# Gate rows by way of a DRAM row and ScalarE's DMA queue, in place of diagonal products on TensorE

## The chip, the cores and the metric

One core of a Trainium2 chip runs the whole program. Its engines are TensorE (PE in the profile; its weight loads are PEld), VectorE (DVE), ScalarE (ACT), GpSimd (POOL) and SyncE (SP). SP and ACT each issue DMAs to a queue of their own (q1 and q10 in the profile), and both queues use the same 16 DMA engines. The metric is the time of one execution on the device in microseconds; three runs of the kernel before took 3442.11, 3445.48 and 3447.05 us, median 3445.48.

## The reference, cut to what matters

Two networks run one after the other, both in fp32, on 256 tokens of 1024 values. The first (two layers of gated FFNs and a mixer of SSD, mLSTM and RWKV heads) is not touched by the change. The second has two layers, works on the 256 tokens and, until its last mixer, on 256 context tokens too, and every branch is scaled by a gate before it is added. The gates are six-fold products of the condition with `ada_w`:

```
m_lat = split((silu_c  @ ada_w[l] + ada_b[l])[:, None, :], 9)     # 9 vectors of 1024, for the tokens
m_ctx = split( silu_cc @ ada_w[l] + ada_b[l], 9)                  # the same for the context
def half_ffn(t, m, j):
    h = modulate(rmsnorm(t, norm_g[l, j]), m[3 * j], m[3 * j + 1])
    return t + 0.5 * m[3 * j + 2] * swiglu_2(h, w_gate, w_up, w_down)
x = half_ffn(x, m_lat, 0);  ctx = half_ffn(ctx, m_ctx, 0)
y_lat, y_ctx = fourier_layer(...)      # layer 0; retention_layer(...) in layer 1
x = x + m_lat[5] * y_lat;   ctx = ctx + m_ctx[5] * y_ctx
x = half_ffn(x, m_lat, 2);  ctx = half_ffn(ctx, m_ctx, 2)
```

A gate is one vector of 1024 values, the same for every token.

## The kernel before, in words

**Where a gate is needed.** A branch's result lies in PSUM with tokens on the 128 partitions and features along the free dimension, 512 to a bank. To scale it, `Gated.vector` (L705) multiplies a bank by `gb`, in which the gate row stands on all 128 partitions, and adds the product to the residual rows. The gates themselves come out of the ada stage (L432) the other way round: `K.mods[:, l, c, n]` holds feature 128c + p of condition n on partition p.

**How the row is spread before.** `Gates` (L648) turns it in pieces of 512 values, here called gate rows. For each, DVE makes four diagonal matrices of 128x128 (`ident` times the column of `mods`, times 0.5 in the half-FFNs, L667), PE multiplies each by a matrix of ones into a bank (`ps`, L681), and ACT copies the bank to `gb` (L691). Six stages have gates: half00, half02 and half10 (the half-FFNs on 512 rows, layer and place in the name) and the Fourier mixer with 2 conditions, so 4 gate rows each; the retention output (tile names ret...) and half12, the last half-FFN, with 1 condition, so 2 gate rows each.

**Order of the work.** Each stage is a generator for each engine, and one list, `order`, fixes how stages alternate: each entry lets one stage take its next step on all four engines (L337). An engine executes its instructions in that order, and a wait holds all that stands behind it on the same engine. In `ffn` (L2953) a step of the half-FFN (one gate-and-up tile: 48 products of 512 columns, or of 256 in half12) is followed by two steps of ada while ada still has work (in half00 and half02), and then by one step of the gates, until these are used up. Fourier and the retention output have their gates' steps written into the order by hand (L3123, L3156).

**Weights.** SP's queue loads tiles of 128x2048 fp32 into a ring of buffers (L319). Each is split in two for PE: ACT writes the high part (`hi`, L310, 1.92 us), DVE the low part (`lo`, L316, 2.29 us), and PE multiplies with both. There are two `hi` buffers in most stages, three in half12. `plan` (L221) puts each split at a place in `order`: `early` before, `late` behind the step of that entry. An ada step on DVE is a set of running sums over a loaded tile (`acc`, L464).

## Time and profile before

| what | value |
|---|---|
| three runs, lowest, median, highest | 3442.11, 3445.48, 3447.05 us |
| profiled execution, first to last instruction (span) | 3442.6 us; no time of its own beside the span is shown, which stands 2.9 us below the median of the runs |
| PE busy | 3305.7 us, 96% |
| DVE busy | 2101.4 us, 61% |
| ACT busy | 1308.7 us, 38% |
| mean granted clock of PE | 0.989 |
| HBM traffic | 459 MB read, 1.05 MB written, 134 GB/s over the span |

Busy time is a share over the whole span; the chain of waits tells which engine set the end. Matmuls overlap one another in the records, so a single duration of a product is longer than the distance to the next one, and the cost of a few products is better read from the distance between marks on either side.

### The profile page before, as it was taken

The numbers are of one execution on the slowest core, as the hardware profiler recorded it, in microseconds if no ns is written. First come the engines' busy times: TensorE is split into PE (matmuls) and PEld (weight loads), VectorE is DVE, ScalarE is ACT, GpSimd is POOL, SyncE is SP. The second block draws the span as 40 slices with busy tenths as digits, with TensorE's granted clock in tenths as the row PEclk, the third lists the DMA queues.
The fourth block names the chain that finished last, engine by engine and source line by source line (L and its number), as shares of the span: only waits on it lengthen the run. The fifth ranks groups of instructions, "written<-read, shape, count | busy, mean of one in ns | idle before, by whom it ended". The sixth has DMA issues, their size and how long they took to land.

```text
span 3442.6 us, 47741 instructions
## 1 busy us (share of the span) xinstructions
PE 3305.7 (96%) x19896; PEld 2886.8 (84%) x19896; DVE 2101.4 (61%) x2545; ACT 1308.7 (38%) x1584; POOL 115.9 (3%) x126
## 2 busy tenths in 40 slices
PE   7998999999999899999999999999999999999998
PEld 7988887998988888798888877888878888787897
DVE  6767657777776667678774855763353333544654
ACT  4444244444435234544421223322232222444443
POOL 0001200000000211000000000000000000000000
PEclk9999999999999999999999999999999999999999
DMA  6542021565553022455443531343222222323452
GB/s 247 235 178 74 27 96 67 204 239 197 236 208 117 27 71 74 171 230 217 147 165 122 179 119 38 134 141 104 87 93 90 93 97 73 126 99 109 165 184 98
DMA packets 83842, 463.08 MB, mean 135 GB/s; under 512 B 7573, under 2 KB 11285, under 8 KB 43562
## 3 DMA queue, kind: packets, MB, share of 16 engines
q1 hardware_dynamic: 77952, 451.45, 35.9%
q10 hardware_dynamic: 5674, 8.57, 0.8%
q8 instruction: 157, 2.57, 0.3%
q14 instruction: 59, 0.48, 0.0%
HBM read 458.95 MB, written 1.05 MB: 134 GB/s over the span
## 4 chain that ended last, share of the span: by engine, by line
PE 66%; DVE 24%; ACT 6%; issue 2%; DMA 0%; POOL 0%; DVEq 0%; ACTq 0%; POOLq 0%
PE ps L100 66%; DVE lo L316 8%; DVE acc L464 5%; ACT hi L310 3%; PE ps L557 1%; DVE acc L461 0%; DVE m0restMs L2004 0%; DVE m1restMs L2004 0%; DVE xt L712 0%; DVE ct L712 0%; DVE half00fin L710 0%; DVE f20rot L886 0%; DVE f21rot L886 0%; DVE f10rot L886 0%; DVE f11rot L886 0%
## 5 line engine op out<-in xcount | busy, mean ns | idle before, releaser
L316 DVE TENSOR_TENSOR lo<-raw,hi 128x2048 fp32r<-128x2048 f32 (+1 forms) x357 | 809.6, 2268 | 627.9 <-ACT hi L310 606.2
L310 ACT ACTIVATE hi<-raw 128x2048 fp32r<-128x2048 f32 (+1 forms) x357 | 676.0, 1894 | 578.1 <-PE ps L100 547.5
L464 DVE SCALAR_TENSOR_TENSOR acc<-raw,sil,acc 128x512 f32<-128x512 f32 x504 | 379.0, 752 | 20.4
L100 PE MATMUL ps<-half00hs,hi 128*128 128x512 f32 x672 | 209.4, 393 | 0.9 <-DVE lo L316 0.9
L100 PE MATMUL ps<-half02hs,hi 128*128 128x512 f32 x672 | 209.1, 392 | 1.0 <-DVE lo L316 1.0
L100 PE MATMUL ps<-half10hs,hi 128*128 128x512 f32 x672 | 208.5, 391 | 1.0 <-DVE lo L316 1.0
L100 PEld LDWEIGHTS ps<-half10hs,hi 128*128 128x128 f32 x672 | 125.7, 188 | 28.5 <-DVE lo L316 1.9
L100 PEld LDWEIGHTS ps<-half02hs,hi 128*128 128x128 f32 x672 | 125.5, 188 | 28.6 <-DVE lo L316 1.9
L100 PEld LDWEIGHTS ps<-half00hs,hi 128*128 128x128 f32 x672 | 125.1, 188 | 28.0 <-DVE lo L316 1.8
L100 PE MATMUL ps<-half02hs,lo 128*128 128x512 f32 x352 | 137.9, 392 | 0.0
L100 PE MATMUL ps<-half00hs,lo 128*128 128x512 f32 x352 | 137.6, 391 | 0.0
L100 PE MATMUL ps<-half10hs,lo 128*128 128x512 f32 x352 | 137.5, 391 | 0.0
L100 PE MATMUL ps<-half12hs,hi 128*128 128x256 f32 x704 | 127.2, 283 | 2.1 <-DVE half12hs L636 2.1
L100 PE MATMUL ps<-hi,half00hf 128*128 128x512 f32 x352 | 110.7, 394 | 2.1 <-DVE mods L474 1.4
L100 PE MATMUL ps<-hi,half02hf 128*128 128x512 f32 x352 | 110.4, 394 | 1.5 <-DVE mods L474 1.5
L100 PEld LDWEIGHTS ps<-half12hs,hi 128*128 128x128 f32 x704 | 109.3, 191 | 3.0 <-DVE half12hs L636 1.8
L100 PE MATMUL ps<-hi,half10hf 128*128 128x512 f32 x352 | 109.2, 390 | 0.0
L100 PE MATMUL ps<-f10hs_h,hi 128*128 128x256 f32 x352 | 101.5, 288 | 7.3 <-DVE lo L316 7.2
L100 PE MATMUL ps<-f21hs_h,hi 128*128 128x256 f32 x352 | 100.9, 287 | 5.5 <-DVE lo L316 3.8
L100 PE MATMUL ps<-msk 128*128 128x128 f32 x886 | 104.5, 276 | 1.0 <-PE ps L2819 1.0
L100 PEld LDWEIGHTS ps<-msk 128*128 128x128 f32 x886 | 102.4, 192 | 3.3 <-PE ps L2819 1.2
L100 PE MATMUL ps<-f20hs_h,hi 128*128 128x256 f32 x352 | 100.8, 286 | 3.2 <-DVE f20hs_l L636 1.5
(921 smaller groups left out, 8019.5 us busy)
## 6 DMA issues: line engine op xcount, KB each, us to landing
raw<-in_ffn_w_gate_up SPq DMA_DIRECT2D x88, 1024.0 KB, 9.0
raw<-in_ffn_gu SPq DMA_DIRECT2D x88, 1024.0 KB, 4.8
raw<-in_ffn_w_down SPq DMA_DIRECT2D x85, 1024.0 KB, 5.2
raw<-in_ada_w SPq DMA_DIRECT2D x72, 1024.0 KB, 4.9
raw<-in_w_in_t SPq DMA_DIRECT2D x28, 1024.0 KB, 4.9
raw<-in_ret_w_in SPq DMA_DIRECT2D x24, 1024.0 KB, 4.8
raw<-in_w_out SPq DMA_DIRECT2D x16, 1024.0 KB, 4.9
raw<-in_w_in_n SPq DMA_DIRECT2D x12, 1024.0 KB, 4.8
```

The source lines that it names most:

```text
L100: return p().matmul(o, l, r, start=start, stop=stop, skip_group_check=True)
L310: a().activation(self.high(w), self.raw[self.place(r)][:, 0:width], ACT.Copy).then_inc(*a.mark(self.wac, w))
L316: v().tensor_tensor(self.low(w), self.raw[self.place(r)][:, 0:width], self.high(w).bitcast(F32), ALU.subtract).then_inc(*v.mark(self.wdv, w))
L464: v().scalar_tensor_tensor(out=acc[:, n, :], in0=w[:, k, :], scalar=s, in1=acc[:, n, :], op0=ALU.mult, op1=ALU.add).then_inc(*v.mark(self. ...
L557: x = p().transpose(b[:, t * 128:(t + 1) * 128], self.xs[:, 2 * s + t, c * 128:(c + 1) * 128], K.ident)
```

## The change

`Gates` no longer uses PE or PSUM. DVE writes the whole gate vector of the stage, scaled, into a small SBUF tile `gcol` (128 partitions, 8 or 16 values of use), once for each stage. ACT's queue writes each condition's 1024 values from there to a row in DRAM, waits until these writes have landed, and then issues one DMA that reads the row or rows back to all 128 partitions of `gb`. The stage that uses the gates waits for that. `Gates` has 2 steps where it had 5 or 3, so the later steps leave `order`; the first two stand where they stood. PE's waits for the gates to have left their bank go, and the DMA scratch of the program is set to 4096 bytes.

```diff
@@ class Core
+        self.gcol = m.take("gcol", 2, 8)
@@ class Gates
-        self.l, self.j, self.rows, self.phases, self.half = l, j, 2 * n, 2 * n + 1, half
-        self.gb, self.dg, self.bank = gb, dg, bank
+    phases = 2
+        self.row = K.nc.dram_tensor(who + "row", (n, 1024), F32, kind="Internal").ap()
+        self.out, self.back = Loads(K.sem(who + "out"), n), Loads(K.sem(who + "back"))
     def vector(self, v):
-        for i in range(self.rows):
-            ...
-            for m in range(4):
-                v().tensor_scalar(self.dg[:, m, :], K.ident, K.mods[:, self.l, c, n:n + 1], self.half, ALU.mult, ...)
-            yield
-        yield
+        if self.before:
+            v.wait_ge(*self.before.out.all)
+        v.wait_ge(*K.ada.dv["mods", 18 * self.l + 17])
+        v().tensor_scalar(K.gcol, K.mods[:, self.l, at:at + 8, :].rearrange("p c n -> p n c"), self.half, None,
+                          ALU.mult).then_inc(*v.mark(self.dv, "gc"))
+        yield
+        yield
-    def tensor(self, p):
-        ...
-            for m in range(4):
-                x = mm(p, b[:, m * 128:(m + 1) * 128], self.K.ones, self.dg[:, m, :])
     def scalar(self, a):
         self.enter(a)
-        yield
-        for i in range(self.rows):
-            a.wait_ge(*self.pe["sum", i])
-            a().activation(self.gb[:, n, q * 512:(q + 1) * 512], self.K.ps[self.bank][:, :], ACT.Copy)...
-            yield
+        a.wait_ge(*self.dv["gc"])
+        for n in range(self.n):
+            a().dma_start(self.row[n].rearrange("(c p) -> p c", p=P), K.gcol[:, n, :],
+                          allow_slow_non_contiguous=True).then_inc(*self.out.mark())
+        yield
+        a.wait_ge(*self.out.all)
+        a().dma_start(self.gb, self.row.rearrange("n k -> (n k)").unsqueeze(0).broadcast_to([P, 1024 * self.n]).rearrange(
+            "p (n k) -> p n k", n=self.n)).then_inc(*self.back.mark())
+        yield
     def done(self, e):
-        e.wait_ge(*self.ac["gb", self.rows - 1])
+        e.wait_ge(*self.back.all)
@@ class Ffn, tensor
-            if self.finish.gates:
-                self.finish.gates.done(p)
@@ class Fourier, tensor
-                    if t == 3:
-                        self.finish.gates.done(p)
@@ network
-    for s in (half, half, four, half, half, four, gates, four, gates, four, four, four, gates, four, gates, four, gates):
+    for s in (half, half, four, half, half, four, gates, four, gates, four, four, four, four, four):
@@ retention output
-        if q < 3:
+        if q < 2:
             run(gates)
@@ kernel
+    nc = _bacc.Bacc("TRN2", target_bir_lowering=False, num_devices=1, dynamic_dma_scratch_size=4096)
```

ACT's instructions at the start of half00, before and after the change (`hi` from `raw` is a weight split, `half00rot` and `half00hf` belong to the half-FFN's first tiles):

```order
L864 ACTIVATE half00hf_241<-half00rot 128x512 [waits s_ffn_act,s_ffn_dve]
L310 ACTIVATE hi_65<-raw_49 128x2048 [waits s_ffn_act,s_ring0,s_norm_dve]
L860 ACTIVATE half00rot<-ps 128x512 [waits s_w_hi,s_ffn_pe]
L864 ACTIVATE half00hf_241<-half00rot 128x512 [waits s_ffn_act,s_ffn_dve]
L691 ACTIVATE half00gb<-ps 128x512 [waits s_ffn_act,s_gate_pe]
L310 ACTIVATE hi_66<-raw_55 128x2048 [waits s_gate_act,s_ring6]
```

```order
L850 ACTIVATE half00hf_241<-half00rot 128x512 [waits s_ffn_act,s_ffn_dve]
L675 DMA half00grow<-gcol 128x8x1 [waits s_ffn_act,s_gate_dve,s_norm_dve]
L675 DMA half00grow<-gcol 128x8x1
L311 ACTIVATE hi_65<-raw_49 128x2048 [waits s_ring0]
L846 ACTIVATE half00rot<-ps 128x512 [waits s_w_hi,s_ffn_pe]
L850 ACTIVATE half00hf_241<-half00rot 128x512 [waits s_ffn_act,s_ffn_dve]
L679 DMA half00gb<-half00grow 128x2048 [waits s_ffn_act,s_half00gout]
L311 ACTIVATE hi_66<-raw_55 128x2048 [waits s_ring6]
```

The two writes, with their wait for DVE's `gcol` (s_gate_dve), stand ahead of a weight split now, and the read back with its wait for the writes (s_half00gout) stands ahead of the next one. The same holds in half02, half10 and half12.

ACT in the retention output, where `ys_h` is the split of the retention's result:

```order
L2433 ACTIVATE ys_h<-retyT 128x1024 [waits s_out_act] x3
L310 ACTIVATE hi_65<-raw_52 128x2048 [waits s_out_act,s_ring3]
L691 ACTIVATE retgb<-ps 128x512 [waits s_w_hi,s_gate_pe]
L310 ACTIVATE hi_66<-raw_53 128x2048 [waits s_gate_act,s_out_pe,s_ring4]
L691 ACTIVATE retgb<-ps 128x512 [waits s_w_hi,s_gate_pe]
```

```order
L2419 ACTIVATE ys_h<-retyT 128x1024 [waits s_out_act] x3
L675 DMA retgrow<-gcol 128x8x1 [waits s_out_act,s_gate_dve]
L311 ACTIVATE hi_65<-raw_52 128x2048 [waits s_ring3]
L679 DMA retgb<-retgrow 128x1024 [waits s_w_hi,s_retgout]
L311 ACTIVATE hi_66<-raw_53 128x2048 [waits s_out_pe,s_ring4]
```

Here too the write comes between `ys_h` and the first split, and the read back between the first split and the second.

ACT in the Fourier stage, from the squares of the second half (`fxs,st<-ct`) on; `fZ` are results of the first transform, `fsin` and `fs_h` belong to the second:

```order
L2621 ACTIVATE fxs,st<-ct 128x512 [waits s_four_act] x4
L2586 ACTIVATE fZ<-ps 128x257 [waits s_four_act,s_four_pe] x4
L2606 ACTIVATE fwx_257<-fwx 5x1024 [waits s_four_act,s_four_second]
L691 ACTIVATE four_gb<-ps 128x512 [waits s_four_act,s_gate_pe]
L2628 ACTIVATE fxs<-ct,st 128x512 [waits s_gate_act,s_four_pool]
L2628 ACTIVATE fxs<-ct,st 128x512 [waits s_four_act,s_four_pool]
L2593 ACTIVATE fsin<-ps 128x256 [waits s_four_act,s_four_pe] x2
```

```order
L2605 ACTIVATE fxs,st<-ct 128x512 [waits s_four_act] x4
L675 DMA fourgrow<-gcol 128x8x1 [waits s_four_act,s_gate_dve]
L675 DMA fourgrow<-gcol 128x8x1
L2570 ACTIVATE fZ<-ps 128x257 [waits s_four_pe]
L2570 ACTIVATE fZ<-ps 128x257 [waits s_four_act,s_four_pe] x3
L2590 ACTIVATE fwx_256<-fwx 5x1024 [waits s_four_act,s_four_second]
L679 DMA four_gb<-fourgrow 128x2048 [waits s_four_act,s_fourgout]
L2612 ACTIVATE fxs<-ct,st 128x512 [waits s_four_pool]
L2612 ACTIVATE fxs<-ct,st 128x512 [waits s_four_act,s_four_pool]
L2577 ACTIVATE fsin<-ps 128x256 [waits s_four_act,s_four_pe] x2
```

The writes stand ahead of the four `fZ` copies, the read back ahead of `fxs` and `fsin`; the three later gate copies are gone.

## Rows read from the trace of the kernel before

**Rows 1.** The page, part 4: engines' shares of the chain that ended last.

```profile
PE 66%; DVE 24%; ACT 6%; issue 2%; DMA 0%; POOL 0%; DVEq 0%; ACTq 0%; POOLq 0%
```

**Rows 2.** The chain in order of time: start, us, what.

```profile
2561.18 175.14 PE ps L100 x782
```

**Rows 3.** Tile half10dg: duration ns min/median/max, first and last start.

```profile
L667 DVE TENSOR_SCALAR half10dg<-msk,mods x16: 285/286/289, 2570.6 to 2606.0; 128x128 f32<-128x128 f32 x16
```

**Rows 4.** Timeline, ACT in half10: start us, us, instruction, [idle before].

```profile
2578.65 0.60 ACT L860 ACTIVATE half10rot<-ps 128x512 f32<-128x512 f32 x1 [6.88 <-PE ps L100]
...
2590.44 0.60 ACT L860 ACTIVATE half10rot<-ps 128x512 f32<-128x512 f32 x1 [7.10 <-PE ps L100]
...
2659.04 0.60 ACT L860 ACTIVATE half10rot<-ps 128x512 f32<-128x512 f32 x1 [6.93 <-PE ps L100]
...
2669.92 0.60 ACT L860 ACTIVATE half10rot<-ps 128x512 f32<-128x512 f32 x1 [6.88 <-PE ps L100]
```

**Rows 5.** Timeline, ACT's queue: DMA issues.

```profile
23.23 0.44 ACTq L413 DMA_DIRECT2D mask<-in_c_mask  x1
...
240.20 0.60 ACTq L1064 DMA_DIRECT2D m0small<-in_rwkv_g_up  x1
```

**Rows 6.** Timeline, half00: ACT, DVE, then PE.

```profile
1671.94 1.92 ACT L310 ACTIVATE hi<-raw 128x2048 fp32r<-128x2048 f32 x1
...
1678.77 1.25 DVE L667 TENSOR_SCALAR half00dg<-msk,mods 128x128 f32<-128x128 f32 x4
1680.13 2.29 DVE L316 TENSOR_TENSOR lo<-raw,hi 128x2048 fp32r<-128x2048 f32 x1
...
1683.18 0.71 PE L100 MATMUL ps<-half00hs,hi 128*128 128x512 f32 x2
...
1696.75 0.71 PE L100 MATMUL ps<-half00hs,hi 128*128 128x512 f32 x2
```

**Rows 7.** Timeline, half02: DVE, then PE.

```profile
2182.69 1.25 DVE L667 TENSOR_SCALAR half02dg<-msk,mods 128x128 f32<-128x128 f32 x4
...
2187.33 0.70 PE L100 MATMUL ps<-half02hs,hi 128*128 128x512 f32 x2
```

**Rows 8.** Timeline, half12: DVE, then ACT.

```profile
3254.53 1.26 DVE L667 TENSOR_SCALAR half12dg<-msk,mods 128x128 f32<-128x128 f32 x4
...
3270.02 0.38 ACT L860 ACTIVATE half12rot<-ps 128x256 f32<-128x256 f32 x1 [2.03 <-PE ps L100]
```

**Rows 9.** Timeline, retention output: ACT, DVE, then PE.

```profile
3187.70 1.92 ACT L310 ACTIVATE hi<-raw 128x2048 fp32r<-128x2048 f32 x1
...
3189.71 1.26 DVE L667 TENSOR_SCALAR retdg<-msk,mods 128x128 f32<-128x128 f32 x4
...
3194.24 0.48 PE L100 MATMUL ps<-hi,ys_h 128*128 128x512 f32 x1
```

**Rows 10.** The DMA view: queues (packets, MB, share), issues (KB each, us to landing).

```profile
q1 hardware_dynamic: 77952, 451.45, 35.9%
q10 hardware_dynamic: 5674, 8.57, 0.8%
...
out<-xt SPq DMA_DIRECT2D x4, 256.0 KB, 2.0
```

**Rows 11.** Timeline, Fourier: ACT, DVE, then PE.

```profile
2059.84 1.34 ACT L2586 ACTIVATE fZ<-ps 128x257 f32<-128x257 f32 x3
...
2066.40 0.72 ACT L2628 ACTIVATE fxs<-ct,st 128x512 f32<-128x512 f32 x1 [1.64 <-POOL st L2709]
...
2068.14 0.86 ACT L2593 ACTIVATE fsin<-ps 128x256 f32<-128x256 f32 x2
...
2069.26 0.42 DVE L2653 TENSOR_TENSOR frot<-ps,fsin 128x256 f32<-128x256 f32 x1
...
2078.98 1.92 PE L100 MATMUL ps<-four_dg,msk 128*128 128x128 f32 x8
2080.68 7.63 PE L100 MATMUL ps<-fd,fhT 128*128 128x257 f32 x32
```

More of the change, by code:

```diff
@@ L648, with __init__ @@
 class Gates(Stage):
-    def __init__(self, K, who, after, l, j, n, half, gb, dg, bank):
+    phases = 2
+    def __init__(self, K, who, after, before, l, j, n, half, gb):
         super().__init__(K, "gate", who, after)
-        self.l, self.j, self.rows, self.phases, self.half = l, j, 2 * n, 2 * n + 1, half
-        self.gb, self.dg, self.bank = gb, dg, bank
+        self.before, self.l, self.j, self.n, self.half, self.gb = before, l, j, n, half, gb
+        self.row = K.nc.dram_tensor(who + "row", (n, 1024), F32, kind="Internal").ap()
+        self.out, self.back = Loads(K.sem(who + "out"), n), Loads(K.sem(who + "back"))
@@ L657, in vector @@
     def vector(self, v):
-        K = self.K
-        self.enter(v)
-        v.wait_ge(*K.ada.dv["mods", 18 * self.l + 17])
-        for i in range(self.rows):
-            n, q = i // 2, i % 2
-            if i:
-                v.wait_ge(*self.pe["sum", i - 1])
-            for m in range(4):
-                c = 8 * (3 * self.j + 2) + 4 * q + m
-                v().tensor_scalar(self.dg[:, m, :], K.ident, K.mods[:, self.l, c, n:n + 1], self.half, ALU.mult,
-                                  ALU.mult).then_inc(*v.mark(self.dv, "dg", i, m))
-            yield
+        K, at = self.K, 8 * (3 * self.j + 2)
@@ L685, in scalar @@
-    def scalar(self, a):
-        self.enter(a)
-        yield
-        for i in range(self.rows):
-            n, q = i // 2, i % 2
-            a.wait_ge(*self.pe["sum", i])
-            a().activation(self.gb[:, n, q * 512:(q + 1) * 512], self.K.ps[self.bank][:, :],
-                           ACT.Copy).then_inc(*a.mark(self.ac, "gb", i))
-            yield
     def done(self, e):
-        e.wait_ge(*self.ac["gb", self.rows - 1])
+        e.wait_ge(*self.back.all)
 class Gated:
@@ L3090, in half_ffn @@
                                     lambda c, v: K.mods[:, l, 24 * j + c, v:v + 1], (l, j), turn))
-        gates = put(name + "g", Gates(K, name + "g", [norm], l, j, nt // 2, 0.5, gb, dg, 6 if nt == 4 else 3))
+        gates = put(name + "g", Gates(K, name + "g", [norm], latest[0], l, j, nt // 2, 0.5, gb))
+        latest[0] = gates
         s = put(name, Ffn(K, name, norm, Gated(gates, rows, K.at(fin, name + "fin", 2, 512)), A["ffn_gu_2"][l, j // 2],
@@ L3118, in network @@
     ffn(half, gates)
-    gb, dg, rot = K.at(49152, "four_gb", 2, 1024), K.at(57344, "four_dg", 4, 128), K.at(59392, "four_fin", 2, 512)
-    gates = put("fourgates", Gates(K, "fourg", [half], 0, 1, 2, 1.0, gb, dg, 7))
+    gb, rot = K.at(49152, "four_gb", 2, 1024), K.at(59392, "four_fin", 2, 512)
+    gates = latest[0] = put("fourgates", Gates(K, "fourg", [half], latest[0], 0, 1, 2, 1.0, gb))
     four = put("four", Fourier(K, "four", half, 0, both, Gated(gates, both, rot)))
-    for s in (half, half, four, half, half, four, gates, four, gates, four, four, four, gates, four, gates, four, gates):
+    for s in (half, half, four, half, half, four, gates, four, gates, four, four, four, four, four):
         run(s)
@@ L3148, in network @@
     ys = K.split(24576, "ys", 16, 256)
-    gb, dg, rot = K.at(57344, "retgb", 1, 1024), K.at(61440, "retdg", 4, 128), K.at(63488, "retfin", 2, 512)
-    gates = put("retgates", Gates(K, "retg", [ret], 1, 1, 1, 1.0, gb, dg, 3))
+    gb, rot = K.at(57344, "retgb", 1, 1024), K.at(63488, "retfin", 2, 512)
+    gates = latest[0] = put("retgates", Gates(K, "retg", [ret], latest[0], 1, 1, 1, 1.0, gb))
     rout = put("retout", Out(K, "retout", [ret], A["ret_w_out_2"][0], yT, ys, Gated(gates, K.xa, rot), 6))
```

13 lines of the change are left out of this document (4 added, 9 removed).

## The prediction

> **What bounds the kernel now.** I read the chain of waits first, then the timeline of TensorE (PE), ScalarE (ACT) and VectorE (DVE) where gate rows are made, then the DMA queues. The chain is 66% PE and 24% DVE [rows 1], and through the whole gated part of a half-FFN it is one unbroken stretch of PE [rows 2]. The reader should take two things from this: a PE instruction removed there shortens the run, and ACT and DVE have slack but lie on the road between a landed weight tile and PE (ACT makes `hi`, then DVE makes `lo`, then PE may start), so anything put ahead of `hi` uses up that slack.
>
> A gate row (512 values spread over 128 partitions) costs four fp32 products on PE, four DVE products of 286 ns (16 in four rows [rows 3]) and one ACT copy beside other work. Four stages make 4 rows each, two make 2: 20 rows. What a row costs on the path is read from the distance of successive `Silu` activations: 11.79 us with a row (2578.65 to 2590.44), 10.88 without (2659.04 to 2669.92), so 0.91 us [rows 4]. I use 0.9.
>
> **What the change puts in.** DVE writes `gcol` (16 columns; I take 0.2 us with its hand-over, since it is smaller than anything shown at 0.286 us). ACT issues one write per 1024 values, later one read back. An issue holds ACT's queue 0.44 to 0.60 us [rows 5]; I take 0.45. Three waits are new, all on ACT, which works in order: the write waits for `gcol`, behind it stand the `hi` split and everything else; the read back waits until the writes landed, and again `hi` stands behind.
>
> *First wait, for gcol.* In half00, `gcol` takes the place of the first diagonal products, at DVE 1678.77, behind the running sums for ada. ACT had long begun its next `hi` at 1671.94 [rows 6]; now that `hi` stands behind the writes. Ready chain: 1678.8 + 0.2 + two issues 0.9 + `hi` 2.0 + `lo` 2.35 (1.92 and 2.29 with their hand-over) = 1684.2, against 1683.18 when PE went on before [rows 6]. So the first row is not a gain of 0.9 but a loss of 1.0; the other three gain 2.7; half00 gives 1.7. In half02 the same 5.45 us from 2182.69 end at 2188.1 against 2187.33 [rows 7]: 2.7 - 0.8 = 1.9. In half10 no ada work is in the way, `gcol` comes at 2570.6 [rows 3] and is ready by 2576.1, before PE needs it (2578.65 [rows 4]): all four rows, 3.6. half12 (`gcol` at 3254.5 [rows 8]) has three `hi` buffers, so there too the delay is covered: 1.8. If that cover were gone in either, each would lose about what half02 loses.
>
> In the retention output projection ACT is done with `ys` and starts `hi` at 3187.70, DVE comes to the gates only at 3189.7, after its `ys` work [rows 9]. The write now waits for it: 3189.7 + 0.2 + 0.45 + 2.0 + 2.35 = 3194.7, against 3194.24: -0.5; the second row gives 0.9: together 0.4.
>
> *Second wait, for the landing.* In DRAM the 8 values of one partition lie 512 bytes apart, and neighbours in DRAM are in different partitions, so no run is longer than 4 bytes: 1024 pieces for a write, 64 for each of 16 DMA engines. Nothing in this trace moves 4-byte pieces. Bounds for one piece: ACT's queue spent 0.8% of 16 x 3442.6 us on 5674 packets, 78 ns each at 1.5 KB; SP's 254 ns (35.9%, 77952 packets) at 5.8 KB [rows 10]. The difference, 41 ns per KB, leaves 17 ns for a packet with no bytes. That is the low end; 78 ns (no saving for being small) I take as the high end of the ordinary, and a slower write to DRAM as a rival below. I choose 50 ns, about the middle. A store of 256 KB lands after 2.0 us [rows 10]. So one write lands after 2.0 + 64 x 0.05 = 5.2 us (3.1 to 7.0), the second of a pair after 2.0 + 6.4 = 8.4 us (4.2 to 12.0).
> The Trainium skill (DMA: Bandwidth & Descriptors, Rules for kernel authors) says a strided last dimension becomes one descriptor per element, and its Specifications table that writes under 512 bytes are done as read-modify-write; no row here shows either. The second speaks against this change and would put a piece above my choice, with no price given. By that page the sum moves towards the slow rival.
>
> Where does the landing matter? In half00 the second write goes out at about 1679.4. Behind the wait come the read's issue, `hi` and `lo`, 4.8 us, and PE wants that tile where its next slot begins: 1696.75 [rows 6], 1.0 later for the first row and 0.9 earlier for the second, 1696.9. So a landing up to 1692.1 is free, 12.7 us; half02 the same. half10: slot at 2590.4 + 0.9 [rows 4] less 1.8 for two rows, 2589.5, less 4.8, less the issue at 2571.2: 13.5. half12: the tile is for the slot whose predecessor ended at 3270.0 [rows 8], less 1.8, less 4.8, less the issue at 3254.9: 8.5 for its single write. At 50 ns all are free. Retention: issue 3189.9 + 5.2 + 0.45 + 2.0 + 2.35 = 3199.9, PE is through its tile at 3194.7 + 5.45 = 3200.15 (24 products of 512 columns, at the 0.227 us each that 10.88 us for 48 of them give [rows 4]): free, by only 0.3 us.
>
> The Fourier stage is different. The writes go out before the `fZ` copies at 2059.84 (their 0.9 us is covered: `fZ` was a backlog), the second at 2060.2. Landing: 2068.6. Behind it stand the read's issue 0.4, two `fxs` (2066.40 to 2068.14, 1.75 us) and `fsin` 0.45, and only then can DVE start `frot`: 2071.2, against 2069.26 [rows 11]. From there to 2078.5 the chain runs through DVE and ACT alone, so this is a loss of 2.0. Against it: the second to fourth gate row leave PE's path, 1.5 (2078.98 to 2080.68 less a restart [rows 11]) + 0.9 + 0.9 = 3.3. The first ended under another wait. Net 1.3.
>
> The read back is wanted when the stage adds its result, in retention 30 us later and elsewhere more, against the 2.0 us of a store [rows 10]: nothing. The banks freed in PSUM and the smaller DMA scratch move no time.
>
> **Sum.** 1.7 + 1.9 + 3.6 + 1.8 + 0.4 + 1.3 = 10.7 us. The span 3442.6 becomes 3431.9; the median shown lies 2.9 us above the span, so 3445.5 - 10.7 = 3434.8. Removing 20 x 0.9 = 18 us of PE thus gives back less than two thirds. At 78 ns a piece: Fourier -2.3, retention -1.1, the rest 9.0: 5.6 us.
>
> **Rivals.**
> Quick pieces (17 to 30 ns). The landing is never waited for. Fourier then gains the four DVE products too, 1.2 us: 9.4 + 3.3 + 1.2 = 13.9, so 3431.6. For it: a packet's cost in this trace is nearly all bytes. Against: these are writes of 4 bytes, of which it has none. Chance 0.20.
> Held issue: a DMA of 1024 pieces keeps ACT's queue longer than 0.45 us, say 2 us more for the second of a pair, since it has to wait for the first to be split up. This adds 2 us in half00, half02 and Fourier: 10.7 - 6 = 4.7, 3440.8. For it: issues in a row can take 0.60 instead of 0.44 us [rows 5]; against: that is little. Chance 0.14.
> Slow pieces, and the kernel is slower: the place is ACT's wait for landing with `hi` behind it. Break-even is near 93 ns: there Fourier stands at -4.2, retention at -2.1, and of the other 9.0 half00 and half02 give up 2.4, half10 0.4. At 130 ns a single write lands after 10.3 us, a pair after 18.6: Fourier -8.9, retention -4.4, half00 and half02 -11.8 together, half10 -5.1, half12 -1.8, against 9.0: 23.0 us slower, 3468.5. For it: writes smaller than anything here, several engines writing next to each other in DRAM; against: the store of 256 KB, 2.0 us, shows no slow DRAM. Chance 0.24.
> That PE's time would be turned into idle time everywhere (DVE bound) I give no chance of its own: the chain shows no DVE in the gated slots.
>
> **Numbers.** Forecast (30 to 78 ns, ordinary issue) 0.42, own range 3432 to 3440; quick 0.20; held issue 0.14; slow 0.24. A measurement of this kernel tells about 0.2%, 6.9 us, from no change. More than that is gained below 71 ns without a held issue: 0.20 + 0.36 + 0.01 = 0.57. Within 0.2%: 0.06 + 0.11 + 0.05 = 0.22. Slower by more: 0.21. The range of 8 in 10: 3429 to 3458; it leaves out the far part of the slow rival and little below.
>
> **What the next profile would show.** Right: ACT's two writes in half00 start near 1679.2 (shifted by what came before), `hi` right behind, PE waiting about 1.7 us there for `lo`; in half10 four slots of 10.9 instead of 11.8 us; landing of the writes 5 and 8 us; a wait of 4 to 5 us of ACT in Fourier, ended by a DMA, with `frot` 2 us later. Wrong: landings over 12 us or waits of ACT ended by a DMA in half00 or half02 that PE then shares (slow rival); writes with an issue over 1 us (held issue); no wait in Fourier (quick).

## The result, and the profile after

The changed kernel takes 3480.5 us (median of 4, 3475.6 to 3483.2) against 3444.2 us: ratio 1.0105 with the interval 1.0091 to 1.0119, 36 us slower. The forecast was 3434.8, the range ended at 3458. The same kernel took 3467.9 us when it was measured again later, and its row writes landed about 1.5 us sooner there (s1_after below; it is not on record on which chip the first result was taken). The trace shown here is of the first result.

The chain of waits of the changed kernel, by engine, against [rows 1]:

```profile
PE 64%; DVE 24%; ACT 7%; DMA 2%; issue 2%; DVEq 0%; ACTq 0%; POOL 0%; POOLq 0%
```

DMA had no share and now has 2%: some transfer is waited for. The waits of ScalarE (ACT) from 1600 us on name it (what waited, what it waited for, us in total, times, longest; of those put down to "issue", the 8.19 us in half00 below is the wait for `gcol`):

```profile
ACT hi L311 <- issue: 19.1, 3, 8.3
...
ACT hi L311 <- DMA retgrow<-gcol: 10.7, 1, 10.7
ACT hi L311 <- DMA half00grow<-gcol: 9.4, 1, 9.4
ACT hi L311 <- DMA half02grow<-gcol: 9.3, 1, 9.3
...
ACT fxs L2612 <- DMA fourgrow<-gcol: 8.9, 1, 8.9
...
ACT hi L311 <- DMA half12grow<-gcol: 5.7, 1, 5.7
```

The timeline of half00, ACT and then TensorE (PE), to be laid beside [rows 6]:

```profile
1684.66 1.02 ACTq L675 DMA_DIRECT2D half00grow<-gcol  x2
1685.72 1.92 ACT L311 ACTIVATE hi<-raw 128x2048 fp32r<-128x2048 f32 x1 [8.19 <-issue]
...
1700.43 0.34 ACTq L679 DMA_DIRECT2D half00gb<-half00grow  x1
1700.81 1.91 ACT L311 ACTIVATE hi<-raw 128x2048 fp32r<-128x2048 f32 x1 [9.39 <-DMA half00grow<-gcol]
```

```profile
1690.02 0.74 PE L100 MATMUL ps<-half00hs,hi 128*128 128x512 f32 x2 [1.71 <-DVE lo L317]
1705.10 1.22 PE L100 MATMUL ps<-half00hs,hi 128*128 128x512 f32 x2 [2.14 <-DVE lo L317]
```

The first wait of PE, 1.71 us, is the predicted one (the write stands behind `gcol`, and `gcol` behind the ada sums). The second was not forecast: the read back goes out at 1700.43, 15.3 us after the second write's issue, and the next `hi` stands behind it. What it does beyond standing is in the windows of the same stage (us, busy time and count of PE, its weight loads, DVE, ACT, POOL; then the granted clock, DMA share, GB/s):

```profile
1700.00:1703.00 3.00, 2.97 (x22) 2.68 (x20) 0.24 (x1) 2.10 (x2) 0.00 (x0) 1.00 0.88 240
1703.00:1706.00 3.00, 0.90 (x2) 0.80 (x3) 2.74 (x2) 0.54 (x2) 0.00 (x0) 0.73 0.98 410
1706.00:1709.00 3.00, 3.00 (x8) 2.33 (x8) 2.18 (x5) 2.41 (x2) 0.00 (x0) 0.50 1.00 423
```

From 1706 to 1709 PE is busy all the time and does 8 products in 3 us, where it does 15 from 1712 to 1715 at full clock: the granted clock is 0.50, 1.2 GHz, behind a wait of 2.14 us.

The landings, by the DMA view (KB each, median us from issue to landing), and ACT's queue, against [rows 10]:

```profile
q10 hardware_dynamic: 16938, 13.86, 1.3%
```

```profile
half00grow<-gcol ACTq DMA_DIRECT2D x2, 4.0 KB, 14.3
fourgrow<-gcol ACTq DMA_DIRECT2D x2, 4.0 KB, 10.9
...
retgrow<-gcol ACTq DMA_DIRECT2D x1, 4.0 KB, 12.6
half12grow<-gcol ACTq DMA_DIRECT2D x1, 4.0 KB, 11.3
```

Forecast were 5.2 us for a single write and 8.4 for the second of a pair. The pieces are what the prediction took them for: q10 has 11264 packets more than before [rows 10], 10 writes of 1024 and 1024 of the reads back; with 128 pieces per write (e4_runs32 below) it has 1280 and the same 1024 more. In the Fourier stage no other transfer runs, so the write can be watched alone. ACT's timeline there, then the windows:

```profile
2070.52 1.03 ACTq L675 DMA_DIRECT2D fourgrow<-gcol  x2
2071.59 1.81 ACT L2570 ACTIVATE fZ<-ps 128x257 f32<-128x257 f32 x4 [1.16 <-PE ps L100]
2083.09 0.34 ACTq L679 DMA_DIRECT2D four_gb<-fourgrow  x1
2083.48 1.54 ACT L2612 ACTIVATE fxs<-ct,st 128x512 f32<-128x512 f32 x2 [8.92 <-DMA fourgrow<-gcol]
```

```profile
2071.20:2072.90 1.70, 1.31 (x7) 0.83 (x6) 0.04 (x1) 1.12 (x3) 0.00 (x0) 1.00 0.56 5
2072.90:2083.00 10.10, 8.72 (x42) 6.67 (x40) 3.04 (x6) 1.47 (x3) 1.33 (x2) 1.00 0.00 0
...
2086.00:2102.00 16.00, 10.54 (x32) 7.30 (x33) 9.87 (x21) 6.73 (x13) 0.00 (x0) 0.57 0.11 45
```

The DMA engines are busy for no more than 1.7 us, where I gave two writes 6.4 us at 50 ns a piece: 0.56 x 1.7 us x 16 engines for 2048 pieces is 7 ns each. Then for 10.1 us the trace shows no transfer, and only then is the write reported as landed. So nearly all of the landing lies behind the last piece that the records show. They do not show what fills it; it is not free of the pieces' number either (e14_few), and the queue is held meanwhile (e3_nowait). PE waits 4.90 us for `frot` at 2086.52, and the 16 us after that run at 0.57 of the clock. In half10 the first slots, which had the gate rows, take 11.20 us each; the forecast had 10.9 for them:

```profile
2602.33 0.60 ACT L846 ACTIVATE half10rot<-ps 128x512 f32<-128x512 f32 x1 [4.71 <-PE ps L100]
...
2613.53 0.60 ACT L846 ACTIVATE half10rot<-ps 128x512 f32<-128x512 f32 x1 [3.91 <-PE ps L100]
```

The retention output waits as Fourier does (ACT, PE, window):

```profile
3217.49 0.38 ACTq L675 DMA_DIRECT2D retgrow<-gcol  x1
...
3230.58 3.93 ACT L311 ACTIVATE hi<-raw 128x2048 fp32r<-128x2048 f32 x2 [10.74 <-DMA retgrow<-gcol]
```

```profile
3234.86 0.80 PE L100 MATMUL ps<-hi,ys_h 128*128 128x512 f32 x1 [6.80 <-DVE lo L317]
```

```profile
3230.00:3240.00 10.00, 5.14 (x12) 4.09 (x13) 4.59 (x2) 3.82 (x2) 0.00 (x0) 0.51 0.98 386
```

### The profile page after: what moved, and what is told of

Read it like the earlier page. It is cut to its first block, busy times and chain, and to the rows that moved or that the text cites. A ratio compares the mean times of both kernels' runs of the same rounds, so it can differ in the third digit from the quotient of the medians.

```text
span 3481.3 us, 47285 instructions
## 1 busy us (share of the span) xinstructions
PE 3319.4 (95%) x19736; PEld 2873.1 (83%) x19736; DVE 2079.6 (60%) x2471; ACT 1296.9 (37%) x1564; POOL 115.9 (3%) x126
## 4 chain that ended last, share of the span: by engine, by line
PE 64%; DVE 24%; ACT 7%; DMA 2%; issue 2%; DVEq 0%; ACTq 0%; POOL 0%; POOLq 0%
PE ps L100 63%; DVE lo L317 8%; DVE acc L465 5%; ACT hi L311 3%; PE ps L558 1%; DVE acc L462 1%; DMA half00grow<-gcol 0%; DMA half02grow<-gcol 0%; DMA retgrow<-gcol 0%; DMA fourgrow<-gcol 0%; DVE m1restMs L1990 0%; DVE m0restMs L1990 0%; DMA half12grow<-gcol 0%; DVE xt L700 0%; DVE ct L700 0%
```

## The experiments

The times are medians, the ratios are against the kernel before beside the same runs. e2_free, e3_nowait, e4_runs32, e14_few and e17_runs16 leave out the right gate values (they read an input instead, or put the row in another order) and serve for the time alone. "Old place" means that every tile lies where it lay in the kernel before.

**The parts one by one (all on one chip).**

e1_place: the kernel before, and only the allocation and the scratch of the change.

```diff
+        self.gcol = m.take("gcol", 2, 8)
-    nc = _bacc.Bacc("TRN2", target_bir_lowering=False, num_devices=1)
+    nc = _bacc.Bacc("TRN2", target_bir_lowering=False, num_devices=1, dynamic_dma_scratch_size=4096)
```

> The kernel before, with only the small tile gcol allocated and the DMA scratch set to 4096 bytes: no instruction differs, SBUF addresses move. Theory of the landing (ACT held until the 4-byte writes have landed, with weight splits behind it): 3444 us as before, within 2 us. Rival, placement: in the trace of the changed kernel a product slot of half10 takes 10.99 us each where before they alternated between 10.88 and 11.15, and the retention stage drifts by 4 us with no gate in it. If addresses do that, this kernel takes 3450 to 3460 us and shows even slots.

Measured 3455.6 us, ratio 1.0035 [1.0022, 1.0048]: 11 us for an unused tile of 64 bytes and a smaller scratch. The timeline of its half10 shows where, ACT's `Silu` rows to be read as in [rows 4]:

```profile
2595.10 0.60 ACT L861 ACTIVATE half10rot<-ps 128x512 f32<-128x512 f32 x1 [7.21 <-PE ps L100]
...
2607.00 0.60 ACT L861 ACTIVATE half10rot<-ps 128x512 f32<-128x512 f32 x1 [7.21 <-PE ps L100]
...
2663.78 0.60 ACT L861 ACTIVATE half10rot<-ps 128x512 f32<-128x512 f32 x1 [7.00 <-PE ps L100]
...
2674.77 0.60 ACT L861 ACTIVATE half10rot<-ps 128x512 f32<-128x512 f32 x1 [7.00 <-PE ps L100]
```

A slot (one gate-and-up tile) with a gate row takes 11.90 us instead of 11.79, a late one without a row 10.99 instead of 10.88. No engine does more; the same 48 products take longer.

e2_free: the changed kernel without the writes and the waits for `gcol` and landing; `gb` is filled from an input.

```diff
-            v.wait_ge(*self.before.out.all)
-        a.wait_ge(*self.dv["gc"])
-            a().dma_start(self.row[n]..., K.gcol[:, n, :], ...)
-        a.wait_ge(*self.out.all)
-        a().dma_start(self.gb, self.row...)
+        a().dma_start(self.gb, K.A["ret_w_out_2"][0][0:self.n, :]...)
```

> The changed kernel without the writes and without ACT's wait for gcol; the read back reads rows of an input instead, so the gates are not the right values. What is left of the change is the gain of the removed products, at the changed placement. Landing, queue and disturbance theories all: 14 to 18 us under before plus whatever placement costs, 3426 to 3432 without placement cost, 3440 with 10 us of it.

Measured 3442.2 us, 0.9993 [0.9984, 1.0002]: 13.4 us under e1_place. That is what the removed rows give at this placement, of the 18 to 19 us that the forecast's terms make without any wait. Part of the gap is in half10: its slots without a row take 11.20 us here, so that a row is worth 0.70 us there and not 0.9; in half00 and half02 (11.89 to 10.99) it is worth 0.9.

e3_nowait: the writes and the wait for `gcol` are back; ACT issues a read back of an input and waits for no landing (the stage that uses the gates does, much later).

```diff
-        a.wait_ge(*self.out.all)
-        a().dma_start(self.gb, self.row...)
+        a().dma_start(self.gb, K.A["ret_w_out_2"][0][0:self.n, :]...)
+        e.wait_ge(*self.out.all)                                         # in done()
```

> The changed kernel with its writes and its wait for gcol, but the read back reads rows of an input, so it does not wait for the writes to land (gate values are not the right ones). Landing theory: nearly all of the loss goes, within 5 us of the kernel without writes. Queue theory (ACT waits for gcol behind DVE's sums): still 10 us or more above the kernel without writes. Disturbance theory (the writes hold up the weight loads): weight loads in the retention output still land after 10 to 12 us and PE still waits there.

Measured 3447.2 us, 1.0007 [0.9998, 1.0016]: the issues, the wait for `gcol` and the writes' traffic cost 5 us. Its trace also shows that not waiting does not bring data sooner: in Fourier the read, issued at 2069.44 behind the writes of 2065.4 on the same queue, moves most of its bytes from 2079 to 2081 and lands after 12.2 us, against 6.1 for the same read in e14_few, issued when the writes had landed.

e4_runs32: the changed kernel with all waits; 128 pieces of 32 bytes per row instead of 1024 of 4 bytes (the values lie in another order).

```diff
-            a().dma_start(self.row[n].rearrange("(c p) -> p c", p=P), K.gcol[:, n, :],
+            a().dma_start(self.row[n].rearrange("(p c) -> p c", p=P), K.gcol[:, n, :],
```

> The changed kernel with the row in DRAM in the order of the partitions, so that a partition writes its 8 values as one run of 32 bytes, 128 pieces for 1024 (the gates then stand in another order, values are not right); all waits stay. Theory that the landing is long because of 1024 small pieces: landing falls from 10 to 15 us to 2 to 4 us and the time to within 3 us of the kernel that does not wait. Rival, the landing is the price of any write from SBUF to DRAM behind loads: landing stays near 10 us and the time near 3480.

Measured 3444.1 us, 0.9999 [0.9990, 1.0008]. The landing wait is gone because the landing is short (1.5 us in Fourier, below); the bytes are the same. ACT still waits for `gcol`, and yet this is 3.1 us under e3_nowait: 4-byte writes seem to cost a little even where ACT does not wait for them. How was not found out.

**The size or the number of the pieces.** e14_few writes 128 of the 1024 pieces of 4 bytes, e17_runs16 writes 256 pieces of 16 bytes.

```diff
+            a().dma_start(self.row[n, 0:128].rearrange("(c p) -> p c", p=P), K.gcol[:, n, 0:1],   # e14_few, and the
+        a().dma_start(self.gb, K.A["ret_w_out_2"][0][0:self.n, :]...)                           # read back as in e3_nowait
+            a().dma_start(self.row[n].rearrange("(a p c) -> p a c", p=P, c=4), ...                # e17_runs16
```

> The changed kernel writing only the first 128 numbers of each row, as 128 pieces of 4 bytes where there were 1024, with the wait for the landing kept; it reads the gate rows from an input instead (their values are others). Theory (it is the number of pieces, not their size): the landing is 1.4 to 4.8 us as with 128 pieces of 32 bytes, and the time about 3444 us as in e4_runs32. Rival (a write of 4-byte pieces lands 9 us or more later whatever their number): landing 9 to 15 us and 3470 to 3480 us.

> As e4_runs32, the row written in pieces of 16 bytes (256 of them; the values lie in another order) where there were 128 of 32 bytes; all waits kept. Measured so far in the Fourier stage, where no other transfer runs: 128 pieces of 32 bytes land after 1.4 and 1.5 us, 128 of 4 bytes after 6.4 and 7.8, 1024 of 4 bytes after 9.7 and 12.1. Theory (what costs the first 5 us is a write of pieces below 32 bytes, whatever their number): 7 to 9 us in the Fourier stage, and 3452 to 3458 us. Rival (it is 4-byte pieces alone): 1.5 to 3 us, and 3444 us.

The Fourier writes in the DMA view, of e14_few, e17_runs16 and e4_runs32:

```profile
fourgrow<-gcol ACTq DMA_DIRECT2D x2, 0.5 KB, 7.1
```

```profile
fourgrow<-gcol ACTq DMA_DIRECT2D x2, 4.0 KB, 2.3
```

```profile
fourgrow<-gcol ACTq DMA_DIRECT2D x2, 4.0 KB, 1.5
```

e14_few took 3454.6 us (1.0029 [1.0019, 1.0039]), e17_runs16 3443.5 us (0.9998 [0.9988, 1.0007]). As many pieces as in e4_runs32, but of 4 bytes, land 5.6 us later; eight times as many of them another 2.5 to 3.8 us (9.6 in s1_after, 10.9 in the first profile). Twice as many of 16 bytes cost 0.8 us. Both of my expectations for e14_few were half right, and mine for e17_runs16 fell: it is the 4-byte piece, more than the number. 8 bytes were not tried, and smaller pieces also bring more partitions' values next to each other in DRAM; no run separates the two.

The number counts as well. On the chip of e14_few, e10_warm2 (below) has all 1024 pieces: 8.8 us against 6.4 for the first Fourier write and 11.0 against 7.8 for the second. With 56 pieces more for each of the 16 engines in the first and 112 in both, that is 43 and 29 ns of landing per piece and engine, though the records show a piece busy for 7 ns.

**The scratch.** e16_scratch is the kernel before with the second half of e1_place's edit alone.

```diff
+    nc = _bacc.Bacc("TRN2", target_bir_lowering=False, num_devices=1, dynamic_dma_scratch_size=4096)
```

> The kernel before with the smaller DMA scratch (4096) alone, and no gcol: every tile lies where it lay. e1_place had both and took 11 us more. Theory (it is the 64 bytes of gcol, behind which every tile of the network moves up, that change the pitch of TensorE's products): 3444 us, as before. Rival (it is the scratch): 3452 to 3457 us.

3444.7 us, 1.0001 [0.9992, 1.0011]. So the 11 us of e1_place are gcol's 64 bytes, behind which the later tiles move up (the tile without the scratch was not run).

**Placement beside the change.** e5_oldplace lays gcol in unused columns of the statistics tile and leaves the scratch at its default.

```diff
-        self.gcol = m.take("gcol", 2, 8)
+        self.gcol = self.st[:, 64:80].rearrange("p (n c) -> p n c", c=8)
```

> The changed kernel with its whole gate row path kept, but with the 16 columns of gcol laid inside the statistics tile and the DMA scratch back at its default size, so that every other tile lies where it lay in the kernel before. Theory (the time is a sum: placement +11.2 us, rows won -13.4, wait for gcol and writes +5, wait for the landing +33): placement is independent of the rest, so this run takes about 3480.5 - 11.2 = 3469 us. Rival (the placement mattered only for the kernel before, and the changed kernel's loss is all in its waits): no change, 3480 us.

3450.9 us, 1.0024 [1.0012, 1.0036], 29.6 us under the changed kernel and not 11. Neither expectation holds. Of the 29.6 us, 12.6 turned out to be the first result's own, as the same kernel took that much less later (s1_after), and 15.6 the placement beside the landing wait (s2_oldplace).

e6_rightruns: the 32-byte runs of e4_runs32 in the old place, with VectorE reading `gb` through a strided view, which puts the values right.

```diff
+        g = self.gates.gb[:, t // 2, :].rearrange("p (q c) -> p c q", c=8)[:, 4 * h:4 * h + 4, :]
```

> As e5_oldplace, with the row written in partition order (32-byte runs, 128 pieces where there were 1024 of 4 bytes) and the product with the gate reading gb through a strided view, so that each column gets its own gate again. Theory (4-byte pieces are what makes the landing long; with 32-byte runs it is 1.4 to 4.8 us and hidden but for the wait for gcol): e4_runs32's 3444.1 less the placement's 11.2 is 3433 us, below the kernel before by 11 us, if the strided read costs VectorE nothing that counts. Rival (the strided read of the gate slows VectorE's 512-column products, which stand on the path at the last column part of each stage): 3436 to 3445 us.

3462.0 us, 1.0046 [1.0033, 1.0058]: slower than with 4-byte pieces. The rival was right, and more so than I put it: 64 such products of 0.45 us more each are 29 us of VectorE. The product with the gate in e6_rightruns (busy us, mean ns; idle before), against 692 ns in the changed kernel:

```profile
L698 DVE TENSOR_TENSOR half00fin<-ps,half00gb 128x512 f32<-128x512 f32 x16 | 18.3, 1143 | 12.5 <-PE ps L100 10.8 <-DVE ct L700 0.5
```

The Trainium skill (SBUF — State Buffer, Door 1: The DMA port swizzle) says that fp32 may be read at a stride of up to 4 numbers for free and pays beyond; at a stride of 8 these rows agree, 451 ns more for 512 numbers.

**Where the landing wait stands.** e8_later issues the read back two of the gates' steps later.

```diff
-    phases = 2
+    phases = 4
...
+        yield
+        yield
         yield
         a.wait_ge(*self.out.all)
...                                   # and the later steps of the gates in the order
```

> The changed kernel with 4-byte pieces and its placement kept, but the read back is issued two steps of the gates' phases later, where the landing (9.7 to 15.3 us) is over. Theory (the 33 us are ScalarE standing in the wait for the landing, and what TensorE then loses): nearly all comes back, about 3447 us, as in e3_nowait, which had no wait. Rival (what costs is the writes' traffic, which holds up weight loads, and not the wait on ScalarE): 3470 us or more.

3447.0 us (median of 10, one of which took 4500.6), 1.0008 [0.9999, 1.0017]: the same 4-byte writes, and nobody waits for them.

**The clock.** e9_warm and e10_warm2 fill PE's waits with idle products (128x128, into a bank that nobody uses); e10_warm2 has half as many.

```diff
+                if not k and self.key in ("half00", "half02") and j in (2, 3):
+                    K.idle(p, 6, 7 if j == 2 else 9)                # e9_warm: 13, 16
+                if 23 <= n <= 27:
+                    K.idle(p, 7, 19 if n == 23 else 4)              # e9_warm: 38, 8
...                                                                  # retention 27, half12 11; e9_warm: 55, 22
```

> The changed kernel with all its waits, and idle products (a 128x128 product into a bank that nobody uses, 0.12 us each) put in TensorE's stream at the places where it stands and waits: 13 and 16 ahead of the third and fourth weight tile of half00 and half02, 38 and four times 8 in the Fourier stage, 55 in the retention's output, 22 in half12. They fill the wait and compute nothing. Theory (of the 33 us of the landing wait some 18 are the idle time of TensorE itself, and the other half is products run at a granted clock of 0.5 to 0.75 behind each wait): the half-clock stretches behind them go, and the time falls by 10 to 15 us, to 3466 to 3471 us. Rival (the clock behind the waits costs little, all is standing): 3478 to 3483 us, or more by what the idle products overrun.

> e9_warm with half as many idle products at each of its places (7 and 9, 19 and four times 4, 27, 11), so that they last about as long as TensorE's waits in the changed kernel (an idle product takes 0.235 us: in e9_warm they took 3.1 and 3.8 us where the waits were 1.7 and 2.1, and 8.7 us where the wait was 4.9, some 22 us too much in all). Theory (the products behind each wait run at a granted clock of 0.5 to 0.75, which costs 10 to 17 us on top of the standing): 3464 to 3472 us. Rival (the clock behind the waits costs little): 3478 to 3483 us.

e9_warm: 3485.9 us (1.0122 [1.0108, 1.0136]). The theory's 3466 to 3471 was missed. I had taken 0.12 us for an idle product; its trace shows 0.235 us for each, so the fill overran the waits of the first profile by some 22 us. The second Fourier write landed after 10.5 us here, near s1_after's 10.8 and not the first profile's 12.1, so the run to compare is s1_after, 18 us below, and the overrun hides what the clock gave back. e10_warm2: 3468.1 us (1.0065 [1.0050, 1.0081]), 12.4 us under the changed kernel's first result, as the theory wanted; but its landings were shorter too (11.0 us).

**One chip for all of it.** The changed kernel and those of three earlier runs once more, together (s1_after is the changed kernel, s2_oldplace is e5_oldplace, s3_warm is e10_warm2, s4_later is e8_later).

> The changed kernel once more, unchanged, on one chip beside e5_oldplace, e10_warm2 and e8_later. In the first profile its second Fourier write landed after 12.1 us; in e5_oldplace, e9_warm and e8_later, all in another call, after 10.4 to 10.5. Theory (the landing is the same for the same kernel, whatever the chip): 3480 us again, 12.1 us in Fourier. Rival (chips differ in this landing by 1.5 us, and so in the time): 10.4 us in Fourier, waits of TensorE near 1 us in half00 and half02, and 3462 to 3472 us.

> e5_oldplace once more, on the same chip as s1_after: the placement of the kernel before, all waits kept. Theory (placement costs 11 us on its own, and the rest of the 29.6 us between e5_oldplace and the changed kernel was a shorter landing): 10 to 13 us under s1_after. Rival (the old placement itself shortens the landing waits): 25 to 30 us under s1_after.

> e10_warm2 once more, on the same chip as s1_after. Theory (the clock behind the waits costs about 12 us where the waits are 2 us and more): 10 to 14 us under s1_after if its waits are as in the first profile, 3 to 8 us if its landings are 1.5 us shorter. Rival (the gain of e10_warm2 was a shorter landing on its chip): same as s1_after.

> e8_later once more, on the same chip as s1_after: the read back two steps later, so no landing wait. Theory: 3447 us as before, whatever the chip, since nobody waits for the landing; the difference to s1_after is what the landing wait costs on this chip. Rival (the chip slows other things too): above 3450 us.

| | us | ratio to before |
|---|---|---|
| s1_after | 3467.9 | 1.0067 [1.0051, 1.0083] |
| s2_oldplace | 3452.3 | 1.0023 [1.0013, 1.0032] |
| s3_warm | 3463.6 | 1.0057 [1.0042, 1.0072] |
| s4_later | 3445.5 | 1.0001 [0.9992, 1.0011] |

s1_after and s3_warm have four runs each, the others ten. s1_after has the time of its rival and nearly the landing (10.8 us for the second Fourier write), s4_later is as expected, and s2_oldplace, 15.6 us under s1_after, lies between its theory and its rival. s3_warm is 4.4 us under s1_after, inside its theory's 3 to 8, but the intervals of the two overlap, so the times alone do not rule out its rival.

The changed kernel is 12.6 us faster here than at first. The waits of ACT and of PE in s1_after, to be laid beside those of the first profile:

```profile
ACT hi L311 <- DMA half00grow<-gcol: 7.8, 1, 7.8
ACT fxs L2612 <- DMA fourgrow<-gcol: 7.6, 1, 7.6
ACT hi L311 <- DMA half02grow<-gcol: 7.6, 1, 7.6
```

```profile
PE ps L100 <- DVE lo L317: 17.4, 14, 5.8
PE ps L2504 <- DVE frot L2638: 6.0, 4, 3.4
```

In the first profile the last two stood at 23.2 and 7.6 us. Landings 1.5 us shorter took 7.4 us from PE's waits. The other 5 of the 12.6 are open: the time lost at a low clock, as summed below, is only 1.6 us less. In s4_later the same two are:

```profile
PE ps L100 <- DVE lo L317: 9.4, 11, 1.8
...
PE ps L2506 <- DVE frot L2640: 0.8, 1, 0.8
```

So the landing wait costs 22.4 us on this chip by the medians (s1_after less s4_later). The two profiled runs are 28.9 us apart in their spans (3470.1 and 3441.2). Of these, 13.2 us are PE's waits (17.4 + 6.0 - 9.4 - 0.8). Most of the rest is the clock: I sum, over windows of 4 us from 1600 to 3460, PE's busy time times what the granted clock lacks to 1. That gives 24.1 us in s1_after, 10.9 in s4_later and 15.6 in s3_warm (25.7 in the first profile, 14.0 in e9_warm, 13.8 in e10_warm2, 9.1 in the kernel before): 13.2 us more with the landing wait than without it, and 8.5 more than with the waits filled. Not all of it stands right behind a landing wait; s1_after has windows at 0.50 to 0.64 at 1660 and at 2156 to 2176 too, and these move from one execution to the next. The windows of the Fourier stage, s1_after and then s3_warm (its counts include the idle products):

```profile
2082.00:2098.00 16.00, 10.79 (x35) 7.61 (x36) 9.75 (x20) 7.02 (x14) 0.00 (x0) 0.59 0.07 28
```

```profile
2082.00:2098.00 16.00, 14.11 (x92) 12.66 (x91) 10.18 (x21) 7.30 (x15) 0.00 (x0) 1.00 0.09 36
```

With the wait filled the clock stays at 1.00. s3_warm's idle products, sized for the first profile, are some 6 us longer than the waits of this chip (1.6 in half00, 2.1 in half02, 1.0 in the Fourier stage, about 1.4 in the last two), and yet it is 4.4 us under s1_after. By these medians the clock is worth about 10 us, an estimate that is uncertain by some 3 us with four runs each; the sums above say 8.5. How much of e10_warm2's 12.4 us was the clock and how much a shorter landing stays open.

**Better versions.** e11_later_old is e8_later in the old place. e12_later_first also runs the gates' step ahead of the two ada steps in the half-FFNs:

```diff
                 run(s)
+                first = gates and j >= late and gates[0].key[-1] == "g"
+                if first:
+                    run(gates.pop(0))
                 if s.nt == 4:
                     fill(2)
...
+                if gates and j >= late and not first:
```

> e8_later (4-byte pieces, the read back two steps later) at the placement of the kernel before (gcol inside the statistics tile, the scratch at its default). Theory (the sum holds: rows won -13.4 us, wait for gcol and the writes' traffic +5, no landing wait): 3434 to 3438 us, faster than before. Rival (placement was worth 11 us only beside the old gate rows): 3444 to 3448 us.

> e11_later_old, and in the half-FFNs the gates' step is put ahead of the ada's two, so that gcol is computed before VectorE's eight ada sums of 6.3 us and ScalarE no longer waits 8.2 us for it. Theory (the wait for gcol costs 1.7 to 1.8 us in each of half00 and half02): 3 to 4 us under e11_later_old, about 3432 us. Rival (the cost beside the landing wait is the writes' traffic): same as e11_later_old.

e11_later_old: 3434.6 us, 0.9971 [0.9960, 0.9983], as its theory had it. e12_later_first: 3429.7 us, 0.9955 [0.9943, 0.9968], 15 us faster than the kernel before and 5.0 under e11_later_old, where 3 to 4 were expected. ACT's timeline in half00 of e12_later_first:

```profile
1669.61 1.52 ACTq L675 DMA_DIRECT2D half00grow<-st  x2
1671.17 1.92 ACT L311 ACTIVATE hi<-raw 128x2048 fp32r<-128x2048 f32 x1 [2.58 <-issue]
1679.34 0.60 ACT L848 ACTIVATE half00rot<-ps 128x512 f32<-128x512 f32 x1 [6.25 <-PE ps L100]
...
1690.22 0.60 ACT L848 ACTIVATE half00rot<-ps 128x512 f32<-128x512 f32 x1 [6.89 <-PE ps L100]
```

`hi` waits 2.58 us instead of 8.19, and the second slot is 10.88 us long, as without a gate row.

## Why the prediction was wrong

The way from the forecast to the result. Each step is the difference of two runs; the first two runs are on different chips, and the sizes hold in this order only:

| | us | runs |
|---|---|---|
| forecast | 3434.8 | |
| rows, `gcol` wait, issues; no landing wait, old place | 3434.6 | e11_later_old |
| wait for the landing | +17.7 | s2_oldplace |
| 64 bytes of gcol | +15.6 | s1_after |
| the first result's own, with landings some 1.5 us longer | +12.6 | the first result |

That e11_later_old meets the forecast to 0.2 us is in part luck. It has no landing wait, where the forecast's sum holds one of 2.0 us in Fourier, and the removed rows gave 13.4 us (e2_free) and 15.1 (e12_later_first, which has hardly a wait left) where the forecast's terms make 18 to 19.

**Right: the price of a row in most slots, the first wait, and where the landing would hurt.** A row is worth 0.9 us in half00 and half02, and in half10 at the old place (its slots there are 10.88 us in e12_later_first, [rows 4]); at the changed placement it is 0.70 in half10. The first wait in half00 and half02, behind the ada sums, is there as told. It was priced at 3.6 us in all (a row of 0.9 lost and 0.8 to 1.0 beyond, twice); taking it away gave 5.0. Held issue, one rival, showed in one place of the changed kernel only, and small: the second issue takes 0.61 us in half00, half02 and Fourier, and 1.06 in half10 (1.20 in s1_after), whose slots stay even.

**Wrong: "So one write lands after 2.0 + 64 x 0.05".** The term that failed is the base, 2.0 us. I took it from a store of 256 KB [rows 10]; for 4-byte pieces it is 5 to 6 us more (e14_few against e4_runs32, 5.6 us), nearly all of it with no transfer in the trace. The term per piece was not too small: the landing grows by 29 to 43 ns per piece (e14_few against e10_warm2), near the 50 I chose. That a piece kept a DMA engine busy for 7 ns only, under the low end of my bounds, shows that busy time was no measure of this term; by it the quick rival would have come true. I had bounded the slope from both sides and the base not at all. The signs given for the slow rival came, landings over 12 us in half00 and half02 and ACT's waits for them that PE shares. The slow rival named the right place and a price of 23 us, and s1_after is at 3467.9 where it said 3468.5; but that is a coincidence, since its second write of a pair landed at 18.6 us (10.8 to 13.7 measured there) and it left out the placement and the clock.

The base alone does not carry the time out of the range. The landings of the first profile (15.3 us for the second write in half00 and half02, 12.7 in half10, 12.1 in Fourier, 12.6 and 11.3 for the single writes of retention and half12), put into the forecast's own terms, give -0.9 - 0.7 + 3.6 - 1.0 - 6.7 - 2.4 = -8.1 us (half00, half02, half10, half12, retention, Fourier), so 3453.6 us, still inside the range. The two terms that were put at nothing do the rest: 15.6 us of placement, and 11.3 that are left, which are of the size of the clock's price. At the old place the same working with s2_oldplace's landings gives 3446.7, against 3452.3 measured.

The Trainium skill (DMA: Bandwidth & Descriptors, Anatomy of one DMA) says, of the DMA path of GpSimd, that most of the fixed cost is the receipt of the last write from the target memory, and that HBM is the slowest target. The 10.1 us without traffic behind the writes agree with that in kind, though no run shows that it is the receipt; its about 2 us agree with the 16- and 32-byte pieces alone (2.3 and 1.5). Its rule that writes under 512 bytes are read-modify-write, which the prediction quoted, does not by itself tell 4 from 16 bytes, both being under it; the runs do.

**Wrong: "the smaller DMA scratch move no time".** The term of the sum for it was nothing. Of the scratch that is true (e16_scratch). The allocation ahead of it in the same diff was not looked at: gcol's 64 bytes move the later tiles, and the distance of PE's products changes with them: a slot of 48 takes 10.99 us against 10.88 late in half10, and 11.20 in its first five, which take 10.88 at the old place (e12_later_first). It costs 11.2 us by itself (e1_place), about as much again beside the late read (10.9 to 12.4, s4_later and e8_later against e11_later_old), and 15.6 beside the landing wait; why 3 to 5 more there is open, and with four runs of s1_after it is not far from the noise. Which tile's address matters was not found out.

**Left out: the price of a wait of PE beyond its length.** In the first profile PE waits 2 us and more behind a landing in five places (2.14 in half00, 2.06 in half02, 4.90, 6.80, 2.89 in half12), and products at a clock of 0.50 to 0.67 follow each; in s1_after there are two (3.44 in Fourier, 5.81 in retention), and behind the 1.67 us of half12 the clock stays at 1.00. The price is some 8 to 13 us by the traces of s1_after, s3_warm and s4_later, part of which stands elsewhere. The prediction's break-even counted standing only. The Trainium skill (TensorE: Matmul & The Clock Gate, HAM oscillation) warns of waits on DMA that leave the next products at the lower clock; the windows above agree, 0.57 and 0.51 behind 4.90 and 6.80 us.

**How long a landing is free** was priced near enough. Half10, free up to 13.5 us by the forecast, kept even slots with a landing of 12.7 us. Half00, free up to 12.7, showed a wait of PE of 0.55 us at 13.7 (s1_after) and 2.14 at 15.3. Half12, free up to 8.5, showed 1.67 at 10.1 and 2.89 at 11.3, and retention, free up to 5.5, showed 5.81 at 11.7 and 6.80 at 12.6. So the mechanism of the second wait was right in every stage. Half00 and half02 lay just at their thresholds, where 1.5 us more of landing are paid nearly in full.

## What to carry to other kernels

A small write that somebody waits for is priced by its size of piece, and its base has to be bounded as well as its slope: here 16 bytes were enough, and so was waiting two steps later; and it is issued ahead of the long work. A price per piece read from busy time is not a price of landing. Before trusting a diff's time, run its allocations alone; here 64 bytes in the memory map cost as much as the idea gained. A wait that is only nearly covered lets a kernel's time move with a landing that is not the same each time, and a long one costs PE its clock on top.

## What was not expected of the hardware

- Two writes to DRAM of 128 pieces of 4 bytes each land after 7.1 us in the median, of 256 of 16 bytes after 2.3, 128 of 32 bytes after 1.5, in a stretch with no other transfer.
- Measured again later, the same 4-byte writes landed 0.9 to 2.5 us sooner (10.9 and 9.6 in the Fourier stage, 14.7 and 13.0 in half02), while the kernel before took 3444 us both times. The second Fourier write took 12.1 us in the first profile and 10.4 to 11.0 in every later one with all 1024 pieces and the wait, on three chips. Whether the chip does it is not shown.
- A read that ACT issues behind 4-byte writes on its queue is held up with them: 12.2 us in e3_nowait against 6.1 in e14_few.
- The distance of PE's products depends on where the tiles lie: 48 of them in 10.88 or in 10.99 us, with no other difference (e1_place).
- VectorE's product of 512 columns takes 1143 ns instead of 692 with one operand read at a stride of 8 numbers.
